# Two-block transformer kernel on one core: another order of the second block's projections and attention groups

## The chip, the cores and the metric

The kernel runs on one core of one Trainium2 chip. The metric is the device time of one execution in microseconds (us); lower is better. All weights come from HBM, every product runs on TensorE (PE), and VectorE (DVE), ScalarE (ACT), GpSimd (POOL) and the DMA queue of SyncE (SP) serve it.

## The reference

Two residual blocks on x of 512 tokens by 1024 features. The first block has a recurrent layer and a sliding-window attention layer; the change leaves its code as it is. The second block, cut to what matters:

```python
h = rms_norm(x, norm_mix) @ w_in                       # 1024 -> D_PROJ
# NSA, 4 heads: compressed, selected and window branch, gated sum
kv_c = gelu(windows(kv[0:2]) + pe, cmp_w1) @ cmp_w2    # 31 compressed keys and values
o = g0 * attn(q, kv_c) + g1 * attn(q, k_sel, v_sel) + g2 * attn(q, k_win, v_win)
# dilated, 2 heads: three groups of keys (every 1st, 4th, 16th), merged by denominators
# stick breaking, 6 heads, strictly causal:
z = q @ k.T * scale
after = reverse_cumsum(log_sigmoid(-z)) - log_sigmoid(-z)
a = exp(log_sigmoid(z) + after);  o = a @ v
x = x + concat(o_nsa, o_dil, o_stick) @ w_out
x = x + relu(rms_norm(x, norm_mlp) @ w_up) ** 2 @ w_down
```

## The kernel before, in words

**Units.** The weights are 173 units of 128 by 1024 floats, in the order in which PE uses them. SP loads unit u into slot u % 4 of a ring, from the first attention on POOL splits it into a high and a low part (`wh`, `wl`), and both wait until PE is done with unit u - 4. Every projection is a three-term product (high by high, high by low, low by high; lines L1017 to L1019). A feature-major tile (`F`, 128 features by 512 tokens) takes one unit and 24 matmuls; a token-major group (`G0` to `G4`, four token tiles) takes four units and 96 matmuls.

**Before the second attention.** PE goes through `G0` (NSA queries, keys, values), the sum of squares, `G1` (dilated queries and gates), the spread of the norm (L1076), `F0` (raw compressed keys), `G2` (dilated keys), `F1`, the hidden layer of the compression (`hid`, four units `U_W1` of short products), `F4`, the turn of the hidden layer (`hT`), six tiles of transposes of the NSA heads (`nT`), `G4` (stick values) and `kc`. Each result stands in one of 8 PSUM banks, and PE may write a bank once the tile before in it was read (`free`): by ACT, or, for `F` and `nT`, by DVE, whose low parts (L1998, L2001, L2020) come behind ACT's high parts (L1543, L1558). DVE normalises heads at L1980 (NSA, wanted by `nT`) and L1976 (dilated, `normalise`).

**The second attention** (`make_attention(2)`) runs over 68 groups of 128 queries: 24 stick groups, 4 compressed (`cmp`), 32 selected or window (`sel`, `win`), and last 8 dilated (`dil`). At step i each engine does a fixed list, in order. PE: `scores(i + 4)` (L666), `turn(i)` (transposes of the probabilities, L683), `values(i - 1)` (L705), a pair's turn (L715), and a piece of an item. ACT: `soft1(i + 3)`, `soft2(i + 2)`, its copies. DVE: `mask1(i + 3)` (L890, softmax kinds), `mask2(i + 2)` (L904, L905, L909, stick kinds), `copy_out(i)` (L822), `finish`, items. Scores have three banks in turn, transposes two, sums of values two. A softmax group needs one pass on DVE and one on ACT, a stick group three and four. `ITEMS2` lays pieces of other work between the steps: the tiles `F2`, `F5`, `F3`, `F6` (stick heads), `G3` (dilated values) and the six turns `dT` of dilated heads (L1298). All of them use bank 7, as the pairs' turns do.

The batches stand in the order stick pair 0, compressed, stick pair 1, NSA pair 0, stick pair 2, NSA pair 1, dilated; the output projection (`output_tile`) and the MLP follow.

Of the kernel before, what the change touches and what calls it, by code (L numbers as in the profile page):

```python
# [20 lines left out]
F32 = mybir.dt.float32  # L21
F32R = mybir.dt.float32r
ALU = mybir.AluOpType
# [3 lines left out]
P = 128  # L27
# [25 lines left out]
U_G1 = U_G0 + 4  # L53
U_F0 = U_G1 + 4
U_G2 = U_F0 + 1
U_F1 = U_G2 + 4
U_W1 = U_F1 + 1
U_F4 = U_W1 + 4
U_G4 = U_F4 + 1
U_FB = U_G4 + 4  # L60
U_FC = U_FB + 2
U_G3 = U_FC + 2
U_OUT2 = U_G3 + 4
# [18 lines left out]
def source_unit(u):  # L82
# [10 lines left out]
    if U_F1 <= u < U_F4:  # L93
        return u + 4 if u == U_F1 else u - 1
    if U_FC <= u < U_OUT2:
        return u + 4 if u < U_G3 else u - 2
# [15 lines left out]
for _name, _n in [("rg", NG * 3 * NRG), ("g_a", KD), ("g_kv", KD), ("g_b", KD), ("g_mix", KD), ("g_mlp", KD),  # L112
# [23 lines left out]
A_OT2, A_BIAS4, A_VC4, A_HIDT, A_BIASD = 12160, 13696, 14208, 14464, 14720  # L136
# [16 lines left out]
EVAC = {"gate": "D", "kcT": "A", "F": "D", "G3": "A", "dT": "A"}  # L153
# [6 lines left out]
MIX_TILE = {0: 10, 1: 2, 2: 6, 3: 0, 4: 9, 5: 11}  # L160
MIX_ORDER = (3, 4, 0, 5, 1, 2)
# [5 lines left out]
SLOT2 = (0, 1, 2, 1, 0, 2)  # L167


def plan():  # L170
# [8 lines left out]
    seg2 += [("G1", t, "A") for t in range(4)] + [("rstd", 2, "B"), ("F", 0, "D")]  # L179
    seg2 += [("G2", t, "A") for t in range(4)] + [("F", 1, "D"), ("hid", 0, "A"), ("hid", 1, "A"), ("F", 4, "D")]  # L180
    seg2 += [("hT", 0, "A")] + [("nT", j, "D") for j in range(6)] + [("G4", t, "A") for t in range(4)] + [("kc", 0, "A")]
    bank, free, before = {}, {}, {}
    count = {"A": 0, "D": 0}
    for seg, items in ((seg1, ITEMS1), (seg2, ITEMS2)):
        for i, (name, j, who) in enumerate(seg):
            key = (name, j)
            bank[key] = i % 8
# [7 lines left out]
            before[key] = free[seg[i - 8][:2]] if i >= 8 else None  # L195
# [5 lines left out]
    last = {i % 8: free[seg2[i][:2]] for i in range(len(seg2))}  # L201
# [3 lines left out]
def attention_one():  # L205

    batches = [dict(kind="swa", head=h, pair=h // 2, half=h % 2, last=h % 2 == 1,
                    turn=h // 2) for h in range(16)]
    groups = [dict(b=h, n=n, w=[128 if n == 0 else 256]) for h in range(16) for n in range(TB)]
    return batches, groups  # L210


def attention_two():
# [10 lines left out]
    batches = stick(0) + cmp_ + stick(1) + nsa(0) + stick(2) + nsa(1) + dil  # L224
    groups = []
    turn = 0
    for b, batch in enumerate(batches):
        batch["turn"] = turn
        turn += batch["last"]
        for n in range(batch["first"], batch["first"] + 2) if batch["kind"] == "cmp" else range(TB):  # L230
# [1950 lines left out]
```

## Time and profile before

| | us |
|---|---|
| median of 3 runs | 1229.95 (1229.75 to 1231.45) |
| profiled execution, own time | 1230.32 |
| its span | 1228.5 |
| PE busy | 1148.0 (93%) |
| DVE, POOL, ACT busy | 630.7, 490.8, 427.2 |

The span runs from the first to the last instruction; 1.8 us of the execution's time lie around it. Busy PE time counts an instruction's full duration, at whichever clock was granted, so a stretch at the lower clock looks busy and does half the work.

### The profile page before, as it was taken

The page shows a single profiled execution, that of the slowest core. Times are in us where ns is not written, and L with a number is a line of the kernel's source. Part 1 is how long each engine was busy: PE and PEld are TensorE (multiplying, and loading weights), DVE is VectorE, ACT ScalarE, POOL GpSimd, SP SyncE. Part 2 cuts the span into 40 slices and gives each one's busy share as a digit, 9 for nine tenths or more (in the row PEclk, how much of TensorE's full clock was granted, in tenths as well). Part 3 has the DMA queues.
Part 4 walks back from the last instruction along what each step waited for, and adds up shares of the span by engine and source line. Part 5 has one row for each costly group of instructions (what it writes and reads, how often), then busy time and mean ns, then how long its engine had stood idle before and what let it go on. Part 6 is the DMA issues. An engine that isn't in the chain of part 4 may idle for free. (4 is left out here: it accounts for less than half of the span.)

```text
span 1228.5 us, 16028 instructions
## 1 busy us (share of the span) xinstructions
PE 1148.0 (93%) x5777; PEld 972.7 (79%) x5777; DVE 630.7 (51%) x1121; ACT 427.2 (35%) x848; POOL 490.8 (40%) x489
## 2 busy tenths in 40 slices
PE   6999999999899989997888887999899999999998
PEld 5888888888788878895777876687688888888887
DVE  6869777585666727138377665334541231231221
ACT  5374586353365602122475554321220110110110
POOL 0000000001614329689521104005877777777772
PEclk9999999999999999998988988569899999999999
DMA  6323232323210103333210001001323323323221
GB/s 251 121 86 96 93 95 95 120 87 103 85 36 19 35 3 118 103 103 121 86 35 19 18 2 69 1 1 51 104 87 102 103 88 100 102 87 101 99 89 51
DMA packets 27277, 97.15 MB, mean 79 GB/s; under 512 B 3024, under 2 KB 3408, under 8 KB 27088
## 3 DMA queue, kind: packets, MB, share of 16 engines
q1 hardware_dynamic: 27216, 96.32, 23.7%
q8 instruction: 40, 0.66, 0.2%
q14 instruction: 21, 0.17, 0.0%
HBM read 94.21 MB, written 2.10 MB: 78 GB/s over the span
## 5 line engine op out<-in xcount | busy, mean ns | idle before, releaser
L476 POOL TENSOR_TENSOR hold<-hold 128x2 f32<-128x2 f32 x117 | 27.9, 238 | 662.9 <-PE bank L1019 662.9
L1017 PE MATMUL bank<-xh,wh 128*128 128x512 f32 x568 | 230.9, 406 | 20.5 <-DVE xl L1645 14.5
L1018 PE MATMUL bank<-xl,wh 128*128 128x512 f32 x568 | 224.6, 395 | 0.0
L1019 PE MATMUL bank<-xh,wl 128*128 128x512 f32 x568 | 224.4, 395 | 0.0
L1017 PE MATMUL bank<-yh,wh 128*128 128x512 f32 x520 | 205.2, 395 | 6.9 <-POOL wl L480 4.9
L1018 PE MATMUL bank<-yl,wh 128*128 128x512 f32 x520 | 204.2, 393 | 0.0
L1019 PE MATMUL bank<-yh,wl 128*128 128x512 f32 x520 | 204.2, 393 | 0.0
L480 POOL TENSOR_TENSOR wl<-raw,wh 128x512 fp32r<-128x512 f32 x117 | 175.3, 1499 | 0.0
L479 POOL TENSOR_TENSOR wl<-raw,wh 128x512 fp32r<-128x512 f32 x117 | 157.5, 1346 | 9.8
L1017 PEld LDWEIGHTS bank<-xh,wh 128*128 128x128 f32 x568 | 108.9, 192 | 45.3 <-issue 14.2
L1019 PEld LDWEIGHTS bank<-xh,wl 128*128 128x128 f32 x568 | 108.7, 191 | 23.4
L1018 PEld LDWEIGHTS bank<-xl,wh 128*128 128x128 f32 x568 | 109.1, 192 | 21.6 <-issue 0.7
L477 POOL TENSOR_SCALAR wh<-raw 128x1024 fp32r<-128x1024 f32 x117 | 125.0, 1068 | 0.0
L1017 PEld LDWEIGHTS bank<-yh,wh 128*128 128x128 f32 x520 | 98.7, 190 | 28.2 <-issue 7.8
L1018 PEld LDWEIGHTS bank<-yl,wh 128*128 128x128 f32 x520 | 98.9, 190 | 20.6
L1019 PEld LDWEIGHTS bank<-yh,wl 128*128 128x128 f32 x520 | 98.8, 190 | 20.8
L1609 ACT ACTIVATE arena<-arena 128x512 f32<-128x512 f32 x32 | 20.2, 633 | 247.3 <-DVE arena L2055 247.3
L1017 PE MATMUL bank<-wh,xh 128*128 128x512 f32 (+2 forms) x224 | 86.1, 385 | 15.6 <-DVE arena L1990 6.4
L705 PE MATMUL bank<-arena 128*128 128x64 f32 (+2 forms) x620 | 96.2, 290 | 3.5 <-ACT arena L796 2.0
L705 PEld LDWEIGHTS bank<-arena 128*128 128x128 f32 x620 | 91.9, 217 | 4.6 <-ACT arena L796 2.6
L2067 DVE TENSOR_TENSOR x<-bank,x 128x512 f32<-128x512 f32 x32 | 22.1, 692 | 142.0 <-PE bank L1019 142.0
L1676 DVE TENSOR_TENSOR wl<-raw,wh 128x1024 fp32r<-128x1024 f32 x56 | 68.0, 1222 | 40.0 <-ACT wh L1368 39.6
(235 smaller groups left out, 1803.8 us busy)
## 6 DMA issues: line engine op xcount, KB each, us to landing
raw<-weight_units SPq DMA_DIRECT2D x173, 512.0 KB, 3.4
x<-x_in SPq DMA_DIRECT2D x4, 512.0 KB, 7.8
out_fm<-x SPq DMA_DIRECT2D x8, 256.0 KB, 2.0
arena<-tables SPq DMA_DIRECT2D x1, 1024.0 KB, 11.4
par<-params SPq DMA_DIRECT2D x1, 166.0 KB, 2.4
arena<-swa_table SPq DMA_DIRECT2D x1, 128.0 KB, 12.0
ident<-identity SPq DMA_DIRECT2D x1, 64.0 KB, 9.2
```

The lines of the kernel that those rows point to most:

```text
L476: pool.tensor_tensor(hold[:], hold[:], hold[:], ALU.add).then_inc(held, 1)
L477: pool.tensor_scalar(wh[:, j, :], raw[:, j, :], 1.0, 1.0, ALU.mult, ALU.mult).then_inc(high_done, 1)
L479: pool.tensor_tensor(wl[:, j, 0:512], raw[:, j, 0:512], wh[:, j, 0:512], ALU.subtract)
L480: pool.tensor_tensor(wl[:, j, 512:1024], raw[:, j, 512:1024], wh[:, j, 512:1024], ALU.subtract)\
L705: mm = pe.matmul(out, pt[:, c % slots, j * P:(j + 1) * P], value_ap(g, s_, kb), start=first, stop=total == 0)
L1017: pe.matmul(out, lh, rh, start=start, stop=False)
L1018: pe.matmul(out, lh, rl, start=False, stop=False)
L1019: return pe.matmul(out, ll, rh, start=False, stop=stop)
L1609: act.activation(sq2[:, i % 2, :], up[:, i % 2, :], ACT.Square)
L1676: dve.tensor_tensor(wl[:, u % RING, :], raw[:, u % RING, :], wh[:, u % RING, :], ALU.subtract)\
L2067: dve.tensor_tensor(x[:, m, :], B[4 + m % 4][:], x[:, m, :], ALU.add).then_inc(down_read, 1)
```

## The change

It reorders the second block; no product is added or dropped.

- `F0` stands ahead of `G1`, and `F4` between the second and the third unit of the hidden layer. `hT` stands behind `nT`.
- `G3` takes the place of `G4` ahead of the attention, with `F2`, `F5`, `F3` behind it. `F6` and `G4` stand behind the scores of the first three groups (`behind_scores`). Only the turns `kcT` and `dT` are left in `ITEMS2`, `dT` at steps 22 to 32.
- DVE normalises the dilated heads (`r1`, `r2`) behind the low parts of `nT`, no longer between `F1` and `F4`.
- Six stick groups stand first; then stick and NSA groups take turns, two NSA or compressed groups for a stick group or one for one, and the dilated groups last. All stick batches sum in bank 5, the others in bank 6 (`bank_of`), with a count of finished batches for each bank.
- From step 1 on PE does `turn(i)` and `values(i - 1)` ahead of `scores(i + 4)`; DVE does `finish` ahead of `mask2`, ACT an item ahead of `soft2`.

```diff
-ITEMS2 = {-3: ("F", 2, 4), 1: ("kcT", 0, 1), 2: ("F", 5, 4), 14: ("F", 3, 4), 18: ("F", 6, 4),
-          27: ("G3", 0, 4), 33: ("G3", 1, 4), 41: ("G3", 2, 3), 44: ("G3", 3, 3),
-          49: ("dT", 0, 1), 50: ("dT", 1, 1), 51: ("dT", 2, 1), 52: ("dT", 3, 1), 53: ("dT", 4, 1), 54: ("dT", 5, 1)}
+ITEMS2 = {-1: ("kcT", 0, 1), 22: ("dT", 0, 1), 24: ("dT", 1, 1), 26: ("dT", 2, 1), 28: ("dT", 3, 1), 30: ("dT", 4, 1),
+          32: ("dT", 5, 1)}
...
-    seg2 += [("G1", t, "A") for t in range(4)] + [("rstd", 2, "B"), ("F", 0, "D")]
+    seg2 += [("F", 0, "D"), ("rstd", 2, "B")] + [("G1", t, "A") for t in range(4)]
     seg2 += [("G2", t, "A") for t in range(4)] + [("F", 1, "D"), ("hid", 0, "A"), ("hid", 1, "A"), ("F", 4, "D")]
-    seg2 += [("hT", 0, "A")] + [("nT", j, "D") for j in range(6)] + [("G4", t, "A") for t in range(4)] + [("kc", 0, "A")]
+    seg2 += [("nT", j, "D") for j in range(6)] + [("hT", 0, "A")] + [("G3", t, "A") for t in range(4)]
+    seg2 += [("F", 2, "D"), ("F", 5, "D"), ("F", 3, "D"), ("kc", 0, "A")]
+    seg2 += [("F", 6, "D")] + [("G4", t, "A") for t in range(4)]
...
-    batches = stick(0) + cmp_ + stick(1) + nsa(0) + stick(2) + nsa(1) + dil
+    batches = stick(0) + stick(1) + stick(2) + cmp_ + nsa(0) + nsa(1) + dil
...
+    groups, ahead = sticks[:6], 6
+    for k, group in enumerate(others):
+        groups.append(group)
+        while ahead < len(sticks) and (ahead - 6) * 33 < (k + 1) * 18 - 9:
+            groups.append(sticks[ahead])
+            ahead += 1
+    return batches, groups + dilated
...
                 for i in range(-LOOK - 1, ng + OUT_LAG):
-                    if 0 <= i + LOOK + 1 < ng:
+                    if (a == 1 or i < 1) and 0 <= i + LOOK + 1 < ng:
                         scores(i + LOOK + 1)
+                    if i == -2 and a == 2:
+                        behind_scores()
                     if 0 <= i < ng:
                         turn(i)
                     if 0 <= i - V_LAG < ng:
                         values(i - V_LAG)
+                    if a == 2 and i >= 1 and i + LOOK + 1 < ng:
+                        scores(i + LOOK + 1)
...
+            for q, u in enumerate(U_W1):
+                if q == 2:
+                    f_tile(4)
...
+            turn_hidden()
+            token_major(U_G3, 4, 384, "G3", xh, xl)
+            for j in (2, 5, 3):
+                f_tile(j)
...
+            def behind_scores():
+                f_tile(6)
+                token_major(U_G4, 4, 384, "G4", xh, xl)
```

On DVE, ahead of the attention, these rows stand in a row before; L1980 and L1976 normalise NSA and dilated heads, L1990 with L1998 or L2001 makes `F1` and then `F4`, L2020 are the low parts of `nT`:

```order
L1980 TENSOR_TENSOR arena<-arena,v 128x768 x4
L2005 TENSOR_REDUCE sides<-ident 128x2
L1990 SCALAR_TENSOR_TENSOR arena<-bank,rstd 128x512
L1998 TENSOR_TENSOR yl<-arena,yh 128x512
L1976 TENSOR_TENSOR arena<-arena,v 128x384 x8
L1990 SCALAR_TENSOR_TENSOR arena<-bank,rstd 128x512
L2011 CAST yh<-ident 128x128
L2012 CAST yh<-arena 128x128
L2001 SCALAR_TENSOR_TENSOR yl<-arena,sides,yh 128x512 x2
L2020 SCALAR_TENSOR_TENSOR yh<-bank,hsc,yh 64x512
```

The same place in the change, where the lines have the numbers L2063, L2073, L2081, L2084, L2099 and L2059 (dilated heads):

```order
L2063 TENSOR_TENSOR arena<-arena,v 128x768 x4
L2088 TENSOR_REDUCE sides<-ident 128x2
L2073 SCALAR_TENSOR_TENSOR arena<-bank,rstd 128x512
L2081 TENSOR_TENSOR yl<-arena,yh 128x512
L2073 SCALAR_TENSOR_TENSOR arena<-bank,rstd 128x512
L2084 SCALAR_TENSOR_TENSOR yl<-arena,sides,yh 128x512 x2
L2099 SCALAR_TENSOR_TENSOR yh<-bank,hsc,yh 64x512
L2099 SCALAR_TENSOR_TENSOR yl<-bank,hsc,yl 64x512
L2099 SCALAR_TENSOR_TENSOR yl<-bank,par,yh 128x512 x2
L2101 CAST yh<-ident 128x128
L2102 CAST yh<-arena 128x128
L2059 TENSOR_TENSOR arena<-arena,v 128x384 x8
```

The eight operations on dilated heads moved behind everything that `F4` and `nT` wait for.

On PE, two steps of the attention before, in NSA groups with a piece of `F` between them (L666 scores, L683 transposes, L705 values, L1017 to L1019 the piece in bank 7):

```order
L666 MATMUL bank1<-yh 128x256
L666 MATMUL bank1<-yl,yh 128x256
L683 MATMUL bank4<-ident,arena 128x128 x2
L705 MATMUL bank5<-arena 128x64
L1017 MATMUL bank7<-xh,wh 128x512
L1018 MATMUL bank7<-xl,wh 128x512
L1019 MATMUL bank7<-xh,wl 128x512
...
L666 MATMUL bank2<-yh 128x384
L666 MATMUL bank2<-yl,yh 128x384
L683 MATMUL bank3<-ident,arena 128x128 x3
L705 MATMUL bank5<-arena 128x64 x2
```

Two steps of the change (L762 transposes, L782 values, L745 and L748 scores):

```order
L762 MATMUL bank3<-ident,arena 128x128 x2
L782 MATMUL bank5<-arena 128x64
L745 MATMUL bank0<-yh 128x384
L745 MATMUL bank0<-yl,yh 128x384
L745 MATMUL bank0<-yh,yl 128x384
L748 MATMUL bank0<-yh 128x128
L762 MATMUL bank4<-ident,arena 128x128 x3
L782 MATMUL bank6<-arena 128x64 x2
L745 MATMUL bank1<-yh 128x128
L745 MATMUL bank1<-yl,yh 128x128
```

The scores moved behind the transposes and values of their step, stick and NSA steps take turns, and nothing stands between the steps.

## Rows read from the trace of the kernel before

**Rows 1.** The page: span, busiest engines, granted clock in 40 slices.

```profile
span 1228.5 us, 16028 instructions
...
PE 1148.0 (93%) x5777; PEld 972.7 (79%) x5777; DVE 630.7 (51%) x1121; ACT 427.2 (35%) x848; POOL 490.8 (40%) x489
...
PEclk9999999999999999998988988569899999999999
```

**Rows 2.** Busy time by stretch; columns as the first line names them.

```profile
core 0: us, PE busy (x) PEld busy (x) DVE busy (x) ACT busy (x) POOL busy (x), PEclk, DMA share, GB/s
504.00:528.00 24.00, 21.03 (x110) 20.34 (x108) 5.62 (x11) 4.66 (x14) 15.23 (x18) 0.93 0.27 88
...
556.00:604.00 48.00, 36.97 (x344) 33.47 (x343) 31.47 (x34) 9.32 (x17) 39.59 (x38) 0.86 0.32 100
604.00:763.40 159.40, 130.76 (x822) 119.90 (x821) 102.64 (x279) 92.34 (x250) 34.09 (x35) 0.90 0.10 34
699.00:718.00 19.00, 17.51 (x131) 16.74 (x131) 16.04 (x37) 15.64 (x38) 0.00 (x0) 1.00 0.01 1
763.40:826.00 62.60, 59.01 (x229) 45.69 (x230) 24.13 (x81) 18.76 (x59) 0.00 (x0) 0.56 0.00 1
```

**Rows 3.** Waits of PE from 500 to 764 us: total, times, longest.

```profile
PE bank L666 <- DVE arena L909: 8.4, 5, 3.1
PE bank L1017 <- DVE arena L1990: 7.3, 2, 6.4
PE bank L1298 <- DVE yl L986: 4.6, 1, 4.6
PE bank L1017 <- DVE yl L986: 4.2, 1, 4.2
PE bank L1017 <- ACT arena L1496: 3.0, 1, 3.0
...
PE bank L1017 <- POOL wl L480: 2.5, 1, 2.5
```

**Rows 4.** Timeline of PE: end of `G4`, and a piece of `F2`.

```profile
603.06 0.33 PE L1018 MATMUL bank<-wl,xh 128*128 128x384 f32 x1
603.23 0.34 PE L1019 MATMUL bank<-wh,xl 128*128 128x384 f32 x1
...
605.20 0.40 PE L1018 MATMUL bank<-xl,wh 128*128 128x512 f32 x1
605.43 0.39 PE L1019 MATMUL bank<-xh,wl 128*128 128x512 f32 x1
```

**Rows 5.** Timeline of DVE ahead of `nT` and `G4`: start, duration.

```profile
561.45 6.58 DVE L1980 TENSOR_TENSOR arena<-arena,v 128x768 f32<-128x768 f32 x4
...
568.26 0.69 DVE L1990 SCALAR_TENSOR_TENSOR arena<-bank,rstd 128x512 f32<-128x512 f32 x1
...
570.90 9.80 DVE L1976 TENSOR_TENSOR arena<-arena,v 128x384 f32<-128x384 f32 x8
580.62 0.68 DVE L1990 SCALAR_TENSOR_TENSOR arena<-bank,rstd 128x512 f32<-128x512 f32 x1
...
582.70 2.63 DVE L2001 SCALAR_TENSOR_TENSOR yl<-arena,sides,yh 128x512 fp32r<-128x512 f32 x2 [0.74 <-ACT yh L1543]
585.37 0.76 DVE L2020 SCALAR_TENSOR_TENSOR yh<-bank,hsc,yh 64x512 fp32r<-64x512 f32 x1
```

**Rows 6.** Groups of DVE from 604 to 763.4 us: busy, mean ns.

```profile
L2001 DVE SCALAR_TENSOR_TENSOR yl<-arena,sides,yh 128x512 fp32r<-128x512 f32 x4 | 3.1, 816 | 2.1 <-ACT yh L1543 2.1
...
L1990 DVE SCALAR_TENSOR_TENSOR arena<-bank,rstd 128x512 f32<-128x512 f32 x4 | 2.7, 681 | 0.0
...
L1998 DVE TENSOR_TENSOR yl<-arena,yh 128x512 fp32r<-128x512 f32 x2 | 2.5, 1252 | 0.3 <-ACT yh L1543 0.3
```

**Rows 7.** Busy time in two stretches at the lower clock (columns of rows 2).

```profile
746.50:753.30 6.80, 4.40 (x19) 4.21 (x20) 3.64 (x8) 2.00 (x5) 4.45 (x5) 0.50 0.38 114
766.90:821.50 54.60, 52.07 (x176) 39.34 (x175) 19.88 (x69) 17.05 (x56) 0.00 (x0) 0.50 0.00 0
```

**Rows 8.** Timeline of PE, the wait ahead of a fall of the clock.

```profile
688.19 1.34 PE L705 MATMUL bank<-arena 128*128 128x64 f32 x6 [1.52 <-DVE arena L822]
```

More of the change, by code:

```diff
@@ L194, in plan @@
                 free[key] = (who, j + 1)
-            before[key] = free[seg[i - 8][:2]] if i >= 8 else None
+            earlier = [k for k in (item[:2] for item in seg[:i]) if bank[k] == bank[key]]
+            before[key] = free[earlier[-1]] if earlier else None
         for key in (item[:2] for item in items.values()):
@@ L199, in plan @@
             free[key] = (EVAC[key[0]], count[EVAC[key[0]]])
-    last = {i % 8: free[seg2[i][:2]] for i in range(len(seg2))}
+    last = {bank[item[:2]]: free[item[:2]] for item in seg2}
     return bank, free, before, last
 def attention_one():
-    batches = [dict(kind="swa", head=h, pair=h // 2, half=h % 2, last=h % 2 == 1,
-                    turn=h // 2) for h in range(16)]
+    batches = [dict(kind="swa", head=h, pair=h // 2, half=h % 2, last=h % 2 == 1) for h in range(16)]
     groups = [dict(b=h, n=n, w=[128 if n == 0 else 256]) for h in range(16) for n in range(TB)]
@@ L710, in pair_turn @@
                 def pair_turn(p):
-                    pe.wait_ge(s["fin"], groups[pairs[p]]["b"] + 1)
+                    for b, batch in enumerate(batches):
+                        if batch["pair"] == pair_of[p] and (batch["last"] or batch["kind"] == "dil"):
+                            pe.wait_ge(*fin_of(b))
                     if before7[("pair", p)]:
@@ L822, in pt_copy @@
                 copy(pt[:, c % slots, 0:n], B[3 + c % 2][:, 0:n]).then_inc(s[("pt_even", "pt_odd")[c % 2]], 1)
-            def stick_count(i):
-                return sum(1 for g in groups[:i] if batches[g["b"]]["kind"] == "stick")
             def dve_part(dve, link, item):
                 def bias_part(at, w):
-                    return ar({256: A_BIASD, 768: A_BIAS4}[at], w) if at >= 256 else bias[:, at:at + w]
+                    return ar({256: A_BIASD, 768: A_ST}[at], w) if at >= 256 else bias[:, at:at + w]
                 def make_bias(b):
@@ L917, in finish @@
                     b = batches[bi]
-                    kind, p = b["kind"], b["turn"]
+                    kind, p = b["kind"], turn_of[bi]
                     ended = end_of[bi] + 1
@@ L926, in finish @@
                         dve.wait_ge(s["o_done"], ended)
-                        nsa_turns = [batches[groups[i]["b"]]["turn"] for i in pairs if batches[groups[i]["b"]]["kind"] == "win"]
+                        nsa_turns = [pair_of.index(j) for j in range(2)]
                         for j, turn in enumerate(nsa_turns):
@@ L990, in dve_part @@
                         mask1(i + LOOK)
+                    if a == 2 and 0 <= i - FIN_LAG < ng and i - FIN_LAG == end_of[groups[i - FIN_LAG]["b"]]:
+                        finish(groups[i - FIN_LAG]["b"])
+                    if a == 2 and i in (0, 2):
+                        item(("F", ("scale", "low")[i // 2]))
                     if 0 <= i + LOOK - 1 < ng:
@@ L1551, in _ @@
             stick_high(4)
+            for j in range(6):
+                wait_done(act, ("nT", j))
+                act.activation(q_stack(j) if j < 4 else side((KS_TILE, KW_TILE)[j - 4], 0), B[BANK[("nT", j)]][:], ACT.Copy,
+                               scale=hsc[:, 1:2] if j < 4 else gain("nsa", j - 2)).then_inc(turned_high, 1)
             wait_done(act, ("hT", 0))
```

322 lines of the change are left out of this document (176 added, 146 removed).

## The prediction, made before the run

> **What bounds the kernel now.** I read the page first. PE is busy 93% of the span, and the row of its clock is full but for a dip in slices 18 to 27, about 560 to 830 us [rows 1]. So almost everywhere only less PE work would help, and this change takes none away; it can gain only inside the dip. The busy times by stretch come next [rows 2]. Before 763.4 us, the second attention has PE busy for 130.8 of 159.4 us at a mean clock of 0.90, DVE for 102.6, ACT for 92.3. The 48 us ahead of it have PE busy for 37.0 at 0.86. The dilated groups that follow keep PE busy for 59.0 of 62.6 us, but at 0.56. The waits say who is late [rows 3]: mostly DVE, with 8.4 us for stick groups (L909), 6.4 us for the bank that `F4` holds (L1990), and 4.6 and 4.2 us for bank 7 (L986), where a turn or a piece of `G3` stands in PE's queue with ready work behind it.
>
> Two costs follow: PE's idle time, and the half clock after it. The last wait of [rows 8], 1.52 us, is followed by such a stretch. No engine is saturated in the attention before: PE's work at full clock is 130.8 x 0.90 = 118 us of 159.4, and DVE stands at 64%.
>
> **The change part by part.** All times below are on the profiled execution's axis.
>
> *F0 ahead of G1.* Before, `G1` waits 3.0 us for a bank of `G0` that ACT empties (L1496) [rows 3], and the stretch from 504 to 528 us runs at a clock of 0.93, so 24 x 0.07 = 1.7 us more are lost [rows 2]. `F0` is 24 matmuls at 0.23 us (the step between two starts in [rows 4]), 5.5 us, which lie over the 3.0. `F0` needs nothing from ACT. I take 4.5 us; bounds 3.0 and 4.7.
>
> *F4 inside the hidden layer.* The 2.5 us wait for POOL's split [rows 3] goes: `F4` gives POOL 5.5 us in the middle of four units that PE uses up fast. But PE then meets `nT` sooner, which waits for L1980. That ended at 568.0 [rows 5], so at 563.5 now. The 2.5 are therefore no gain of their own; what counts is DVE's chain.
>
> *Normalising of the dilated heads moved.* Before, its 9.8 us (L1976) stood between the F1 and the F4 work, and `G4` waited for F4's bank [rows 5]. It now runs under `G3`, 16.6 us of PE (96 matmuls at the 0.17 us step of [rows 4]), with the wide `F` tiles behind it. What is late next: `G3`'s second tile needs the bank of the first `nT` tile, whose low part is queued on DVE behind F1 and F4. From 563.5 that queue is: F1's part 2.6 us (568.26 to 570.90), F4's 4.7 (580.62 to 585.33), one low part 0.8, and 0.3 for L2005: 571.9 [rows 5]. `G3` ends at 571.9 + 16.6 = 588.5, and I add 2.4 for the half clock after a wait of some 5 us: 590.9. `G4`, which stood there before, ended at 603.5 [rows 4]. Gain so far 12.6 us, the 4.5 included. Bounds: without the clock's loss 15; with the whole 48 x 0.14 = 6.7 us of it as before [rows 2], 8.
>
> *The pieces moved out of the loop.* Before, four `F` tiles (22 us) and `G3` (16.6) lay between steps, 38.6 us. Now `F2`, `F5`, `F3`, then `F6` and `G4` are one block: 16.5 + 5.5 + 16.6, with about 2 us for `kc` and the first three groups' scores, 40.6 us. The first turn is at 590.9 + 40.6 = 631.5. POOL's splitting keeps up, as it has over 5 us for an `F` unit.
>
> *The loop.* From there 56 steps lead to the first dilated scores, which stood at 763.4. PE's work for all 60 groups is 118 - 39 = 79 us at full clock, 74 for these steps, 1.3 us a step. DVE's is 102.6, less 8.3 for the `F` tiles [rows 6], plus 2.3 for `F6` (one of four L1990, half of L2001), less about 4.5 for three narrow stick groups done under the block (eight stick groups keep DVE busy 16.0 us from 699 to 718 [rows 2]), plus 1.5 for finishing work that comes earlier: 93.6 us. So DVE, not PE, is the bound, and the pieces that covered DVE's lateness are gone: they no longer hide anything but were 38.6 us of PE's path. How well can DVE be used? Lower end: as now, 64%, which makes 146 us. The stretch from 699 to 718, eight stick groups in a row, has 16.04 of 19 us, 84% [rows 2]. Upper end 95%, 98 us. In the new order the three passes of a stick group lie beside softmax groups, whose passes need no ACT between them; and PE's transposes, for which DVE's copies wait, no longer stand behind scores that wait for a bank. I take 86%, just above the stick stretch: 109 us.
>
> The start costs extra. ACT empties `G4`'s four banks and makes F6's high parts before it can touch group 3, and groups 3 to 5 are stick groups in a row. I estimate 4 us (0 to 8). And PE at 1.3 us of work in a step of 1.95 is 68% busy; some of the time the clock will be at half. In such a stretch PE needs 2.6 us a step, 0.65 over DVE's. If a quarter of the steps are so, 14 x 0.65 = 9, of which DVE's own waits absorb part: I take 5 (0 to 18). First dilated scores at 631.5 + 4 + 109 + 5 = 749.5, against 763.4: 13.9 us gained, where 12.6 had been gained ahead of the block.
>
> *Dilated groups and after.* The same work, at the same clock of 0.50 [rows 7]. PE idles 62.6 - 59.0 = 3.6 us there; with turns and values ahead of the scores some is covered: 1.5. The output projection is unchanged.
>
> *New waits.* All NSA batches sum in bank 6, so a batch's first values wait for the `finish` of the batch before, behind which the next scores are queued; before, batches alternated over two banks. There are nine such places. The nearest row is PE's 1.52 us wait for a DVE copy [rows 8]: between 0 and 14 us. PE has slack of 0.65 us a step and DVE is working during those waits, so I count it inside the 86%.
>
> Sum: 13.9 + 1.5 = 15.4 us off 1230.3, 1214.9; the median of the runs shown is 0.4 below the profiled one, so 1214.5, and I say **1214**.
>
> **The rule that speaks against it.** In the dilated stretch PE is busy for 52.1 of 54.6 us and stays at 0.50, so the level of 1.2 GHz, all the way [rows 7]. Its work is fp32 scores, transposes and fp32 values. The loop loses its dense projection pieces and becomes mostly transposes and values as well. The Trainium skill, "TensorE: Matmul & The Clock Gate", Part 4, says that a transpose does not count as PE-busy in the same way for the clock. By that rule the whole loop could sit at 1.2 GHz, 148 us; by my reading of the rows it does not, 109 + 5. Against the rule: from 746.5 to 753.3 PE had only turns, scores, transposes and values, was idle for 2.4 us of it, and the clock came back to full behind it [rows 7].
>
> **Rivals.**
> 1. *The loop turns slow (slower than before).* PE's 74 us at a mean clock c take 74 / c. From 635.5 to 764.9 there are 129 us, so the change loses as soon as c falls under 0.57. At 0.50: 635.5 + 148 = 783.5, 20 us late, less 1.5: 1248. The same comes about if DVE stays at 64%: 635.5 + 146. For it: the dilated stretch, and 68% busy. Against it: the mean of 0.90 now with 18% idle, and a PE at half clock is fully busy again. Chance 0.16.
> 2. *The waits for `finish` are all paid.* Nine times 1.5 us on the path: 14 of the 15 us are gone, 1228. For it: one bank for each kind. Chance 0.05.
> 3. *DVE nearly saturated and the clock holds.* 631.5 + 2 + 98 = 731.5, 32 us earlier, 1196; if the dilated groups also stayed at full clock, up to 20 us below that, but nothing in the rows points to it. Chance 0.18.
> 4. *My forecast*, 1206 to 1226: chance 0.61.
>
> **How the numbers follow.** A measurement of this kernel tells about 0.2%, 2.5 us, from no change: 1227.5 to 1232.4. Faster by more: 0.61 + 0.18 = 0.79. Same: 0.05. Slower: 0.16. The range is 1199 to 1234: it holds the forecast, the nearer part of rival 3, rival 2 and the mildest slow cases. The forecast's own range is 1206 to 1226.
>
> **What would show it.** In the profile after: no wait of 3.0 us for L1496; the wait ahead of the second group after `nT` shorter than 6.4 us and put down to a low part of `nT`; the first transposes of probabilities at about 631; no projection matmul until the dilated groups; the first 64-row scores at about 750; DVE at 80 to 90% in between, and the clock above 0.8. A mean clock below 0.6 or DVE below 70% would make me wrong towards slower; a first 64-row score before 740 towards faster.

## The result, and the profile after

| | before | after |
|---|---|---|
| median, same chip | 1230.70 (1229.75 to 1233.00, 4 runs) | 1244.66 (1243.99 to 1247.33, 4 runs) |
| ratio | | 1.0118, 95% interval 1.0075 to 1.0160 |
| profiled span | 1228.5 | 1245.5 |

The change makes the kernel 1.2% slower, some 14 us; 1214 had been predicted. The page of the kernel after (compare [rows 1]; the dip of its clock is deeper, not wider):

```profile
span 1245.5 us, 16005 instructions
PE 1166.5 (94%) x5777; PEld 988.1 (79%) x5777; DVE 631.4 (51%) x1121; ACT 424.4 (34%) x847; POOL 492.6 (40%) x489
PEclk9999999999999999999977786559899999999999
```

The work is the same, yet PE is 18.5 us busier: its matmuls lasted longer. Busy time by stretch says where (columns of [rows 2]; the fourth row is the loop, from the first transposes of probabilities to the first 64-row scores):

```profile
504.00:528.00 24.00, 24.00 (x127) 22.49 (x126) 12.28 (x19) 4.88 (x14) 19.10 (x19) 1.00 0.28 92
571.70:605.90 34.20, 34.16 (x166) 31.04 (x167) 19.18 (x20) 4.40 (x10) 31.76 (x31) 0.95 0.37 123
605.90:632.10 26.20, 25.92 (x145) 24.40 (x146) 8.70 (x19) 9.81 (x25) 21.19 (x22) 1.00 0.32 102
632.10:783.40 151.30, 113.66 (x613) 102.78 (x612) 89.36 (x256) 78.53 (x220) 2.50 (x2) 0.74 0.02 7
783.40:844.10 60.70, 59.12 (x229) 45.88 (x228) 25.31 (x81) 17.81 (x58) 0.00 (x0) 0.55 0.00 1
```

Everything ahead of the loop went as planned: PE has no gap from 504 to 528 us and 0.3 us of gaps from 571.7 to 632.1. The timeline of PE shows the one long new wait of the front, the first `F2` matmul, the first transposes of probabilities and the first 64-row scores:

```profile
571.74 0.69 PE L1102 MATMUL bank<-wh,xh 128*128 128x384 f32 x1 [3.57 <-DVE yh L2099]
...
589.38 0.39 PE L1102 MATMUL bank<-xh,wh 128*128 128x512 f32 x1
...
632.10 0.51 PE L762 MATMUL bank<-ident,arena 128*128 128x128 f32 x3
...
783.43 1.43 PE L745 MATMUL bank<-arena 64*128 64x128 f32 x5
```

`G3` ends at 589.4 (590.9 forecast), the loop begins at 632.1 (631.5 forecast). Then 151.3 us pass where 118 had been forecast; before, the first 64-row scores stood at 763.4 [rows 2], now at 783.4. In the loop PE idles for 151.3 - 113.7 = 37.6 us, at a mean clock of 0.74, and DVE is busy for 59% of it. Its longest waits, all engines (total, times, longest):

```profile
DVE arena L973 <- PE bank L745: 33.0, 20, 3.8
ACT arena L875 <- DVE arena L992: 29.0, 20, 3.5
ACT arena L857 <- DVE negm L973: 27.0, 27, 2.5
PE bank L782 <- ACT arena L880: 18.8, 10, 4.5
DVE arena L908 <- PE bank L762: 18.1, 4, 14.1
...
PE bank L782 <- DVE arena L908: 10.1, 7, 2.0
```

DVE's `mask1` (L973) waits for scores (L745), ACT's `soft2` (L875) for DVE's `mask2` (L992), PE's value products (L782) for the copy of ACT (L880) or of DVE (L908): a ring, in which everybody waits. (Of the 18.1 us of L908 for L762, 14.1 are one wait.) One turn of the ring, in the timelines of PE, ACT and DVE:

```profile
684.04 0.38 PE L762 MATMUL bank<-ident,arena 128*128 128x128 f32 x2
688.88 0.66 PE L782 MATMUL bank<-arena 128*128 128x64 f32 x2 [4.46 <-ACT arena L880]
689.30 0.45 PE L745 MATMUL bank<-yh 128*128 128x128 f32 x1
```

```profile
684.22 0.19 ACT L857 ACTIVATION_READ_ACCUMULATOR arena<-arena,negm 128x1 f32 x1
687.94 0.63 ACT L875 ACTIVATE arena<-arena 128x512 f32<-128x512 f32 x1 [3.53 <-DVE arena L992]
688.47 0.26 ACT L880 ACTIVATE arena<-bank 128x128 f32<-128x128 f32 x1
```

```profile
684.77 0.42 DVE L1048 TENSOR_TENSOR arena<-arena 128x256 f32<-128x256 f32 x1
685.23 0.69 DVE L987 SCALAR_TENSOR_TENSOR arena<-bank,arena 128x512 f32<-128x512 f32 x1
685.95 1.22 DVE L988 TENSOR_TENSOR_SCAN arena<-ones,arena 128x512 f32<-128x512 f32 x1
687.21 0.69 DVE L992 TENSOR_TENSOR arena<-bank,arena 128x512 f32<-128x512 f32 x1
...
692.61 0.29 DVE L973 CUSTOM_DVE_ANT_0 arena<-bank,arena 128x128 f32<-128x128 f32 x1 [3.31 <-PE bank L745]
```

PE's transposes are done at 684.4. Their copy by ACT (L880) is ready to run then, but it is queued behind `soft2` (L875) of a stick group two ahead, which waits for DVE's three passes (L987 to L992). So the value products start at 688.9, and the scores behind them, which need none of this, are 4.5 us late too, and with them those of the next step, a softmax group. For these DVE then waits 3.3 us, until 692.6.

### The profile page after: what moved, and what is told of

It reads as the page before. It is cut to its first block and busy times, and to the rows that moved or that the text cites. A ratio compares the mean times of both kernels' runs of the same rounds, so it can differ in the third digit from the quotient of the medians.

```text
span 1245.5 us, 16005 instructions
## 1 busy us (share of the span) xinstructions
PE 1166.5 (94%) x5777; PEld 988.1 (79%) x5777; DVE 631.4 (51%) x1121; ACT 424.4 (34%) x847; POOL 492.6 (40%) x489
## 5 line engine op out<-in xcount | busy, mean ns | idle before, releaser
L1102 PE MATMUL bank<-xh,wh 128*128 128x512 f32 x568 | 227.6, 401 | 16.9 <-DVE xl L1728 15.0
L782 PE MATMUL bank<-arena 128*128 128x64 f32 (+2 forms) x620 | 108.9, 316 | 35.0 <-ACT arena L880 18.8
L782 PEld LDWEIGHTS bank<-arena 128*128 128x128 f32 x620 | 102.1, 238 | 42.4 <-issue 12.9
L857 ACT ACTIVATE arena<-arena,negm 128x128 f32<-128x128 f32 (+3 forms) x120 | 61.2, 510 | 82.0 <-DVE negm L973 81.4
```

Source lines behind the costliest of these rows:

```text
L782: mm = pe.matmul(out, pt[:, c % slots, j * P:(j + 1) * P], value_ap(g, s_, kb), start=first, stop=total == 0)
L857: e = act.activation(pr[:, col:col + w], pr[:, col:col + w], ACT.Exp, scale=-1.0, bias=negm[:, ring_of[g["b"]], n:n + 1], accum_out=to_sum)
L1102: pe.matmul(out, lh, rh, start=start, stop=False)
```

## The experiments

The changed kernel differs from the one before in four main things: the front, the pieces (in the loop or ahead of it), the order of the groups, and the order of a step. With them go a bank for each kind of group and the place of `finish` and of an ACT item. **The theory (A)**: scores behind value products close the ring above. **Rivals**: (B) PE's clock is low without dense pieces, whatever the order; (C) the mixed order of the groups is to blame; later (D), the step order harms only where mixed groups meet a loop without pieces.

"Loop" runs from the first transposes or values to the first 64-row scores, "dilated" from there to the output projection, both in the profiled execution; "idle" is the loop less PE's busy time in it. Ratios are against the kernel before on the same chip. Kernels marked "in" keep `F2`, `F5`, `F3`, `F6`, `G3` and `dT` as pieces, "out" have them as the change has. "Batch, out" keeps one bank for all stick batches and one for the others; "batch, in" has the two banks in turn, as before.

| kernel | groups, pieces, scores | median us | ratio (95%) | loop, PE busy, idle, clock | dilated |
|---|---|---|---|---|---|
| before | batch, in, first | 1230 to 1234 | 1 | 146.9, 121.3, 25.6, 0.90 | 63.0 |
| after | mixed, out, last | 1244.7 | 1.0118 (1.0075 to 1.0160) | 151.3, 113.7, 37.6, 0.74 | 60.7 |
| e1 | mixed, out, first | 1225.0 | 0.9941 (0.9918 to 0.9965) | 126.4, 99.7, 26.7, 0.80 | 62.9 |
| e2 | mixed, out, middle | 1220.7 | 0.9867 (0.9786 to 0.9948) | 125.2, 101.7, 23.5, 0.79 | 61.7 |
| e3 | batch, out, last | 1229.1 | 0.9985 (0.9969 to 1.0000) | 131.8, 100.0, 31.8, 0.83 | 61.5 |
| e4 | after + dense products | 1253.5 | 1.0190 (1.0158 to 1.0223) | 154.6, 122.7, 31.9, 0.85 | 61.4 |
| e5 | after, copies first | 1238.9 | 1.0068 (1.0035 to 1.0101) | 146.4, 112.7, 33.7, 0.73 | 54.1 |
| e6 | batch, in, first, new front | 1209.4 | 0.9856 (0.9792 to 0.9921) | 143.6, 119.3, 24.3, 0.92 | 56.7 |
| e7 | before with scores last | 1213.6 | 0.9864 (0.9813 to 0.9915) | 148.0, 126.4, 21.6, 0.88 | 45.4 |
| e8 | mixed, in, first | 1206.0 | 0.9813 (0.9756 to 0.9869) | 145.5, 118.1, 27.4, 0.93 | 56.6 |
| e9 | mixed, in, last | 1223.5 | 0.9927 (0.9899 to 0.9954) | 159.5, 132.1, 27.4, 0.85 | 61.3 |
| e10 | batch, in, last, new front | 1198.3 | 0.9718 (0.9689 to 0.9746) | 147.9, 122.8, 25.1, 0.91 | 45.3 |
| e11 | batch, out, first | 1215.8 | 0.9853 (0.9806 to 0.9900) | 126.7, 101.6, 25.1, 0.78 | 55.7 |
| e12 | before, last in dilated only | 1215.1 | 0.9849 (0.9807 to 0.9891) | 150.6, 126.8, 23.8, 0.86 | 45.4 |
| e13 | e6, last in dilated only | 1197.1 | 0.9747 (0.9684 to 0.9811) | 144.1, 120.3, 23.8, 0.92 | 43.7 |
| e14 | e1, last in dilated only | 1226.9 | 0.9946 (0.9903 to 0.9988) | 136.4, 110.6, 25.8, 0.71 | 55.9 |
| e15 | e8, last in dilated only | 1211.6 | 0.9836 (0.9767 to 0.9905) | 143.9, 120.2, 23.7, 0.93 | 60.9 |
| e16 | e13, middle in the loop | 1195.3 | 0.9722 (0.9661 to 0.9784) | 142.9, 120.6, 22.3, 0.92 | 45.1 |
| e17 | after, finish behind | 1257.3 | 1.0242 (1.0136 to 1.0347) | 159.4, 120.6, 38.8, 0.67 | 61.1 |
| e18 | e15, finish behind | 1221.1 | 0.9936 (0.9895 to 0.9977) | 158.2, 129.9, 28.3, 0.86 | 54.4 |

The kernels were timed in five lots: e1, e3, e4, e6; e2, e5, e7, e8; e9 to e12; e13 to e16; e17 and e18. The kernel before had medians from 1230.1 to 1234.3 in them, so a difference of medians from two lots is open by some 4 us; that holds for most of the small ones below. How much one trace's loop may vary is seen in four pairs that have the same loop program: before and e12 (146.9, 150.6), e6 and e13 (143.6, 144.1), e8 and e15 (145.5, 143.9), e1 and e14 (126.4, 136.4). Only the last is far apart, and its idle time agrees (26.7, 25.8): the 10 us are matmuls that took longer, at a mean clock of 0.71 in place of 0.80. The verdicts below go by medians; the loops say where the time lies.

**e1_scores_first**: the changed kernel with the old step order.

```diff
-                    if (a == 1 or i < 1) and 0 <= i + LOOK + 1 < ng:
+                    if 0 <= i + LOOK + 1 < ng:
                         scores(i + LOOK + 1)
...
-                    if a == 2 and i >= 1 and i + LOOK + 1 < ng:
-                        scores(i + LOOK + 1)
```

> The changed kernel, but PE does scores(i + 4) ahead of turn(i) and values(i - 1) in every step, as the kernel before did. Theory A (the new order of a step couples the engines: values(i - 1) wait for a copy queued behind soft2 or mask2, and the scores that DVE needs next stand behind them): the 33 us that DVE waits for scores shrink below 10, the first 64-row scores come 15 to 30 us earlier than 783, the time falls from 1245 to 1215 to 1230. Theory B (the lost clock: without dense projection pieces PE works at 1.2 GHz in much of the loop): the loop stays within 5 us of now, mean clock still about 0.75, 1240 to 1248. Theory C (the mixed order of the groups does not suit the queues): no change either, 1240 to 1248.

1225.0 us, 20 less than the changed kernel. Its loop by stretch, and its waits:

```profile
631.80:758.20 126.40, 99.66 (x598) 91.59 (x596) 88.11 (x254) 76.34 (x218) 1.72 (x2) 0.80 0.02 7
```

```profile
ACT arena L873 <- DVE arena L990: 28.1, 20, 3.1
PE bank L745 <- DVE arena L990: 17.4, 14, 3.0
```

Against the loop of after, 24.9 us are gone: 10.9 of idle time, 14.0 of busy time, which are the same matmuls at a higher clock. DVE's `mask1` no longer waits for scores at all; ACT's for `mask2` has not changed. PE does wait again for a score bank, the wait that the new step order was to remove, but it costs less.

**e3_batch_order**: the changed kernel, step order kept, groups in the old order of batches.

```diff
-    groups, ahead = sticks[:6], 6
-    for k, group in enumerate(others):
...
+    per = [groups_of(b) for b in range(16)]
+    groups = [g for b in (0, 1, 6, 7, 2, 3, 8, 9, 10, 11, 4, 5, 12, 13, 14, 15) for g in per[b]]
```

> The changed kernel with the groups in the order of the kernel before (stick pair 0, compressed, stick pair 1, NSA pair 0, stick pair 2, NSA pair 1, dilated), all else as changed. Theory C: 1215 to 1232, the loop from 632 to the first 64-row scores falls from 151 to below 135 us. Theories A and B: the stick batches in a row make DVE's chain longer, 1245 to 1260.

1229.1 us, 15.6 less. So with the scores last the mixed order costs nearly as much as the step order does, and the two are not separate terms: that called for the other combinations.

**e4_dense**: the changed kernel with two more products of 512 columns ahead of the scores of groups 4 to 59, without the four compressed ones. What they write is overwritten.

```diff
+                        if a == 2 and kind != "dil" and i > 3:
+                            for _ in range(2):
+                                pe.matmul(score_bank(st)[:], idm[:, 0, :], yh[:, 2, :], start=True, stop=True)
```

> The changed kernel with two extra products of 128x512 (fp32r, about 0.43 us at full clock) into the score bank ahead of each group's scores from group 4 to the last NSA group; their result is overwritten, so the output is that of the changed kernel. It adds 56 x 0.43 = 24 us of PE work at full clock. Theory B: the clock in the loop rises from 0.75 to above 0.9 and the time stays or falls, 1232 to 1247. Theory A: the waits stay and the added work stands in front of the scores, 1250 to 1270, with the clock higher all the same.

104 products at the 0.23 us step of [rows 4] are 23.9 us of work, for 8.9 us of time:

```profile
630.80:785.40 154.60, 122.69 (x710) 108.36 (x710) 88.47 (x251) 76.63 (x216) 1.30 (x2) 0.85 0.01 5
```

The clock rose from 0.74 to 0.85, PE's busy time by only 9 us, its idle time fell by 5.7. Over 60% of the added work paid for itself. The run does not say that the clock is harmless, it says that the ring stays when the clock rises.

**e6_front_alone**: the kernel before with the new front, that is `F0` ahead of `G1`, `F4` inside the hidden layer, `nT` ahead of `hT`, the dilated heads normalised behind.

```diff
-    seg2 += [("G1", t, "A") for t in range(4)] + [("rstd", 2, "B"), ("F", 0, "D")]
+    seg2 += [("F", 0, "D"), ("rstd", 2, "B")] + [("G1", t, "A") for t in range(4)]
...
-            normalise(r1, 6)
-            normalise(r2, 12).then_inc(heads_normed, 1)
...
+            normalise(r1, 6)
+            normalise(r2, 12).then_inc(heads_normed, 1)
```

> The kernel before with only the part ahead of the attention changed: F0 ahead of G1, F4 inside the hidden layer, hT behind nT, the dilated heads normalised behind the low parts of nT; G4 stays there, the loop is that of before with all its pieces. By my sum the part ahead gains 12.6 us (the changed kernel's trace agrees: its first turn is at 632.1 where I had 631.5), so 1215 to 1221. If the loop's start then waits for the normalising instead (9.8 us of DVE now behind nT), half of it comes back: 1221 to 1226.

1209.4 us: the front was worth more than forecast. `kc` ends at 588.1 where it ended at 604.2, 16 us earlier; the rest lies mostly in the dilated section (56.7 after 63.0). Its four runs lie between 1204.4 and 1219.7, so the size is loose.

**e2_scores_mid**: the changed kernel, step order turn(i), scores(i + 4), values(i - 1).

```diff
-                    if 0 <= i - V_LAG < ng:
-                        values(i - V_LAG)
                     if a == 2 and i >= 1 and i + LOOK + 1 < ng:
                         scores(i + LOOK + 1)
+                    if 0 <= i - V_LAG < ng:
+                        values(i - V_LAG)
```

> The changed kernel with a step's order on TensorE turn(i), scores(i + 4), values(i - 1): the scores stand behind the transposes but ahead of the value products. Theory A (the new step order couples the engines: the scores of the group four ahead stand behind value products that wait for ScalarE's or VectorE's copy of the turned probabilities, and both of these engines then wait for those scores): the wait of the values for the copies no longer holds the scores, so most of the 20 us between the changed kernel and the one with its scores first come back, 1225 to 1232 us. Theory B (the loop is long because TensorE's clock is low when transposes and values stand together): the transposes are apart from the values again, loop clock near 0.80 as with the scores first, time 1225 too; it differs from A only if the clock and the time part ways. Theory A2 (it is the transposes ahead of the scores that do the harm, not the values): about 1240 us, little won.

1220.7 us, 24 less than the changed kernel and no more than with the scores first. Its four runs lie between 1204.0 and 1223.6, and its profile is of the slowest; all are at least 20 us under the changed kernel. DVE's wait for scores is 9.0 us here, after 33.0. Transposes ahead of the scores do no harm: it is the value products, which wait for the copies, that must not stand ahead of them.

**e5_copies_first**: in the changed kernel, ACT and DVE copy the turned probabilities ahead of `soft2`, `finish` and `mask2`.

```diff
+                    if a == 2 and 4 <= i < 56:
+                        copy_out(i)
                     if 0 <= i + LOOK - 1 < ng:
                         soft2(i + LOOK - 1)
```

> The changed kernel, TensorE's order as it is, but in steps 4 to 55 ScalarE and VectorE copy the turned probabilities of group i before their soft2, finish and mask2 of other groups. Theory A (the values wait because those copies are queued behind soft2 and mask2, which wait for each other): the waits of L782 for the copies (18.8 + 10.1 us in the loop of the changed kernel) fall under 12 us together, and 8 to 15 us of the time come back, 1230 to 1237 us. Theory B (clock): no product is changed, so the clock is not either, and the time stays within 3 us of 1244.7. Theory C (the copies wait for the transposes now, so what was queued behind them is late instead): 1240 to 1250 us, with a wait of ScalarE's and VectorE's copies for L762 in place of L782's wait.

1238.9, 6 us of the 20. The ring is loosened at another place; PE's idle time falls by 3.9, and `mask1` waits for scores still for 26.4 us.

**e7_before_scores_last**: the kernel before with the new step order alone.

```diff
-                    if 0 <= i + LOOK + 1 < ng:
+                    if (a == 1 or i < 1) and 0 <= i + LOOK + 1 < ng:
                         scores(i + LOOK + 1)
...
+                    if a == 2 and i >= 1 and i + LOOK + 1 < ng:
+                        scores(i + LOOK + 1)
```

> The kernel before, with only the step order on TensorE changed from step 1 on: turn(i), values(i - 1), then scores(i + 4). Units, pieces and the order of the batches stay. Theory A (step order alone couples the engines): slower by 10 to 25 us, 1241 to 1256, with long waits of the value products for copies and of VectorE and ScalarE for score banks. Theory C (the step order only hurts together with the mixed order of the groups; in batch order it cost little in the changed kernel): within 5 us of 1231. Theory B (clock): slower only by as much as the loop's mean granted clock falls from before's.

1213.6, 1.4% faster, which none of the three had. The loop is as long as it was (148.0 after 146.9), as theory C had it; what changed is the dilated section, 45.4 after 63.0.

**e8_all** and **e9_mixed_pieces_last**: e6 with the mixed groups, their banks and `finish` ahead of `mask2`, the pieces kept in the loop (some at other steps); scores first in e8, last in e9.

> The kernel before with the new front (F0 ahead of G1, W1 and F4 interleaved, turns of the NSA heads ahead of the hidden layer's) and the mixed order of stick and sparse groups with its banks, but with the scores first in each step as before and with F2, F5, F3, F6, G3 and the dilated turns kept as pieces in the loop. The front alone gave 1209.4 us. If mixing the groups evens out VectorE's and ScalarE's load (as the prediction had it), it gives 3 to 15 us more: 1194 to 1206. If the mixed order gives nothing because the pieces already filled the waits: 1207 to 1212. If it harms (waits for score banks of mask2 at every other step): 1213 to 1225.

> The kernel with the new front, mixed groups and the pieces kept in the loop (1206.0 us with its scores first, first 64-row scores at 747.0), and now the new step order: scores(i + 4) behind turn(i) and values(i - 1), in front of the piece. Theory A (the new step order harms wherever groups are mixed): first 64-row scores 15 to 25 us later, 762 to 772. Theory D (it harms only where mixed groups meet a loop without pieces, since a piece gives the copies their time before the next values): first 64-row scores within 4 us of 747. The time itself also hangs on how long the dilated section's half clock lasts.

1206.0 and 1223.5: mixing the groups won 3 us over e6, which these intervals do not tell from nothing. The step order on top cost 17.5 by the medians, which are from two lots, and 14 by the ratios and by the loops:

```profile
601.50:747.00 145.50, 118.12 (x766) 107.29 (x764) 98.15 (x260) 77.85 (x220) 32.04 (x31) 0.93 0.09 30
```

```profile
601.00:760.50 159.50, 132.10 (x780) 119.02 (x778) 98.61 (x259) 79.80 (x221) 31.84 (x32) 0.85 0.08 27
```

Here the idle time is 27.4 in both, and the whole 14 us are busy time, the same matmuls at a lower mean clock. The pieces do not save the mixed loop, so theory D falls. The waits of e9 show the ring again; in e8 `mask1` never waits for scores:

```profile
ACT arena L859 <- DVE arena L974: 32.5, 20, 3.6
DVE arena L955 <- PE bank L731: 24.8, 18, 3.2
```

**e10_front_scores_last**: e6 with the new step order, the same edit as in e7.

> The kernel before with the new front alone (1209.4 us with its scores first, first 64-row scores at 745.7, 56.7 us from there to the output projection), and now the new step order. In the kernel before the new step order alone left the loop as long as it was (616.5 to 764.6) and shortened the dilated section from 63.0 to 45.3 us. If both parts add: first 64-row scores at 747, output projection 45 to 57 us later, 1194 to 1207 us. If the gain in the dilated section was chance: 1207 to 1212.

1198.3, 11 us under e6, in the dilated section. In this loop, in batch order, `soft2` waits for `mask2` half as often as in e9:

```profile
ACT arena L779 <- DVE negm L896: 37.1, 28, 4.4
DVE arena L896 <- PE bank L670: 17.1, 17, 3.2
ACT arena L797 <- DVE arena L915: 15.1, 10, 2.5
```

**e11_batch_scores_first**: e3 with the scores first.

> The changed kernel with the groups in the batch order of before and its scores first in each step: of the change only the front, with the pieces out of the loop, is left. With the new step order this order of groups had its first 64-row scores at 762.9 (131.8 us of loop), and with scores first the mixed order had them at 758.2 (126.4). Theory D (step order harms only mixed groups without pieces): within 4 us of 762.9, so mixing alone gives 4 to 5 us where scores stand first. Theory A (step order harms in any order): 750 to 758.

1215.8, 13 us under e3: 5.1 in the loop, all of it idle time and more, 5.8 in the dilated section. The loop's end (760.7) is where theory D had it, and yet the step order cost something here too: batch order without pieces is not safe from it.

**e12_last_in_dilated**, **e13_front_last_in_dilated**, **e14_e1_last_in_dilated**, **e15_all_last_in_dilated**: before, e6, e1 and e8, each with scores last from step 55 on only.

```diff
-                    if 0 <= i + LOOK + 1 < ng:
+                    if (a == 1 or i < 55) and 0 <= i + LOOK + 1 < ng:
...
+                    if a == 2 and i >= 55 and i + LOOK + 1 < ng:
+                        scores(i + LOOK + 1)
```

> The kernel before, with the new step order only for the scores of the eight dilated groups (steps 55 on). Putting every group's scores last gave 1213.6, all of it between the first 64-row scores and the output projection (63.0 to 45.3 us). If that gain comes of the step order in the dilated section itself: 1211 to 1218 us, that stretch under 52 us. If it comes of the clock that the loop ahead leaves, or of chance: 1225 to 1235 us, that stretch 60 to 64 us.

> The kernel before with the new front (1209.4 us; loop 143.7 us with scores first, 147.9 with scores last; dilated section 56.7 and 45.3 us) and the new step order only for the scores of the eight dilated groups. If loop and dilated section are separate terms: first 64-row scores at 745.7, output projection 45 us later, 1192 to 1197 us, the best so far. If the dilated section is short only behind a loop that has scores last too: 1205 to 1212.

> The changed kernel with its scores first (1225.0 us, 62.9 us from the first 64-row scores to the output projection), and the new step order only for the dilated groups. If the step order in the dilated section is what keeps the clock up there: that stretch 45 to 50 us and 1208 to 1213 us. If the clock at entry decides (mixed loop without pieces, TensorE short of work ahead of it, as in the changed kernel's 60.6 us with the same order): 60 to 63 us, 1222 to 1227 us.

> New front, mixed groups, pieces in the loop, scores first (1206.0 us, dilated section 56.6 us), with the new step order only for the dilated groups. With scores last throughout that stretch was 61.3 us. If the step order in the dilated section decides: 45 to 50 us, 1194 to 1200. If the clock at entry decides, and this loop leaves it as the one with scores last did: 57 to 62 us, 1206 to 1212.

1215.1, 1197.1, 1226.9 and 1211.6. Behind the batch loops the dilated section shrinks to 45.4 and 43.7 us; behind the mixed ones the same step order leaves it at 55.9 and 60.9. The dilated stretch of e13 and of e15:

```profile
747.50:791.20 43.70, 40.43 (x225) 32.17 (x224) 24.06 (x81) 18.35 (x59) 0.00 (x0) 0.84 0.00 1
```

```profile
746.80:807.70 60.90, 57.92 (x228) 44.71 (x227) 26.01 (x84) 18.60 (x59) 0.00 (x0) 0.58 0.00 1
```

The same work, 17.5 us of busy time apart. At the start of the stretch, PE's waits in e13 and in e15, whose clock fell at 751.2 and stayed at 0.50 for 51.2 us:

```profile
751.35 0.66 PE L709 MATMUL bank<-arena 128*128 128x64 f32 x4 [0.40 <-ACT arena L802]
```

```profile
748.76 0.41 PE L768 MATMUL bank<-arena 128*128 128x64 f32 x2 [0.70 <-DVE arena L890]
749.87 1.67 PE L731 MATMUL bank<-arena 64*128 64x256 f32 x6 [0.71 <-DVE mtmp L955]
```

**e16_front_mid_then_last**: e13 with the step order of e2 in the loop.

> New front, batch order, pieces in the loop; the loop's steps are turn(i), scores(i + 4), values(i - 1), those of the dilated groups have scores last. Scores last throughout gave a loop of 147.9 us and 1198.3; scores first a loop of 143.7. If only scores behind values cost something, and transposes ahead of scores help: loop 138 to 144 us, 1186 to 1196. If transposes ahead of scores cost as much: loop 147 to 149, 1196 to 1200.

1195.3, the lowest median of all, but with e13 (1197.1) and e10 (1198.3) inside what these runs can tell. All three beat both kernels, by 2.5 to 2.8% of before.

**e17_finish_behind** and **e18_e15_finish_behind**: after and e15 with `finish` back behind the copies on DVE.

```diff
-                    if a == 2 and 0 <= i - FIN_LAG < ng and i - FIN_LAG == end_of[groups[i - FIN_LAG]["b"]]:
-                        finish(groups[i - FIN_LAG]["b"])
...
-                    if a == 1 and 0 <= i - FIN_LAG < ng and i - FIN_LAG == end_of[groups[i - FIN_LAG]["b"]]:
+                    if 0 <= i - FIN_LAG < ng and i - FIN_LAG == end_of[groups[i - FIN_LAG]["b"]]:
                         finish(groups[i - FIN_LAG]["b"])
```

> The changed kernel (1244.7 us), with finish on VectorE back behind copy_out, as before. If finish ahead of mask2 is what makes soft2 and the copies behind it late (1.5 us of five operations at 683.7 to 685.2, ahead of mask2's 2.7 us), the loop gets 5 to 15 us shorter: 1230 to 1240. If the mixed order and the scores behind the values do it, finish is only moved in a row that is late anyway: within 4 us of 1244.7; slower if the values of the next batch then wait longer for fin.

> New front, mixed groups, pieces in the loop, scores first but last in the dilated section (1211.6 us, 61.0 us from the first 64-row scores to the output projection), with finish behind the copies. If finish's place makes the dilated section slow: 44 to 50 us there and 1195 to 1200 us. If the clock that the mixed loop leaves at its end does: 57 to 62 us there, 1206 to 1214 us.

Both got slower, by 12.6 and 9.6 us. `finish` ahead of `mask2` is a gain in the mixed order, where a batch's first values wait for the bank of the batch before. With it behind, this wait of e17 grows from 3.4 us in the changed kernel:

```profile
PE bank L782 <- DVE arena L1048: 17.6, 6, 4.5
```

So the new place of `finish` does not explain the cost of the mixed order or of the step order.

## Why the prediction was wrong

**Ahead of the loop it was right.** The wait for L1496 is gone and the stretch from 504 to 528 runs at full clock; the new wait stood where it was named, 3.57 us on a low part of `nT`; `G3` ended 1.5 us sooner than forecast, the loop began 0.6 us later. The front's gain had been put at 12.6 us (bounds 8 to 15). By the end of `G3` it is 14.1 (603.5 to 589.4), inside them. In e6, with `G4` in that place, it is 16.1 (604.2 to 588.1 at the end of `kc`), a little more.

**The step that failed is the loop**, "86% ... 109 us", and in it the sentence that "PE's transposes ... no longer stand behind scores that wait for a bank". That was counted as a gain, and what the move queued behind the value products was not costed. Value products wait for copies, copies for `soft2`, `soft2` for `mask2`; with the scores behind them `mask1` waits as well. In the changed kernel this is worth 20 us (e1), with pieces in the loop 14 to 17.5 (e9 against e8). Its place is shown by e2, in the mixed order without pieces: the scores may stand behind the transposes, not behind the values. DVE was at 59%, not 86%, and below 70% was the prediction's own sign of being wrong towards slower. With the scores first it is 88.1 of 126.4 us, 70%, so 86% was too high even then.

**The mixed order was counted as a help, and with it the step order costs most.** In batch order with the pieces in, the step order in the loop costs 1.2 us by medians and 3.8 by the loops (e10 against e13); in mixed order 11.9 and 15.6 (e9 against e15). Batch order is not free of it where the pieces are out: there the step order, in the loop and the dilated section together, costs 13 us, of which 5.1 in the loop (e3 against e11). The rows fit: `soft2` waits for `mask2` 20 times in after, e1, e8 and e9, and 9 to 13 times in the batch orders. That more such waits are the cause was argued from them, not tried by itself. Scores first, mixing gains nothing that can be measured with the pieces in (e8 against e6), and loses 9 us with the pieces out (e1 against e11), most of it behind the loop.

**The pieces were not "38.6 us of PE's path".** Taken out of the mixed loop they shorten it by 19.1 us only (145.5 to 126.4), and of the 23.9 us of e4's products 8.9 were paid. In the loop such work fills waits and keeps the clock up (0.93 against 0.80). Ahead of the loop it costs its full time: e1 is 19 us slower than e8, both with scores first.

**The clock term** was 5 us, 0 to 18. Between the loops of after and e1 14.0 of 24.9 us are slower matmuls, between e9 and e8 all 14. So much of what the step order costs is paid through the clock. That rival B alone, a low clock without dense pieces, is not the cause is shown by e1 and e2: they have no pieces either, and are 20 and 24 us faster than the changed kernel. How the same idle time comes with a lower clock in e9 than in e8 stays open. Rival 1 is what came about in time and nearly in its second form, "if DVE stays at 64%": it gave 783.5 or 781.5 for the first 64-row scores and 1248, and 783.4 and 1244.7 were measured. Its first form, a mean clock under 0.57, did not happen (0.74). The waits for `finish` of rival 2 came to 5.5 us of the 14 (3.4, 1.4 and 0.7). The rule weighed there (the Trainium skill, "TensorE: Matmul & The Clock Gate", Part 4: a transpose does not count as busy time in the same way), read as strictly as the prediction read it, would have put the whole loop at 1.2 GHz; the trace shows a mix of both levels in every loop without pieces, with means of 0.67 to 0.85. e4 leaves the rule possible as a part of the cause: dense products raised the clock, but they also filled idle time, so it doesn't tell one from the other.

**The sum** of the steps from before to after, by the first 64-row scores of the profiled executions: front -17.7 (e6), mixed groups +1.4 (e8), pieces out +11.2 (e1), step order +25.3 (after), in all +20.0; by medians 1231, 1209.4, 1206.0, 1225.0, 1244.7. The step order had been forecast as a gain and the moved pieces as nearly neutral, and what the front gave hid half of the loss. The dilated stretch, where 1.5 us were forecast as gained, took 60.7 us after 63.0.

**What stays open** is the clock of the dilated section. With its own scores last it kept the full clock for 22 to 25 us behind the batch loops with pieces (e7, e10, e12, e13, e16); in every other kernel the clock had fallen by some 5 us after the first 64-row scores. All this is one profiled execution of each kernel; the single runs of e6 (1204.4 to 1219.7) and e2 leave room for either course in the same program. Short waits at its start, 0.70 and 0.71 us against 0.40, stand ahead of the fall in e15; no run changed them alone. e18, at 54.4 us, lies between. The bank for each kind and the place of the ACT item were tried only together with other parts of the change, so their shares of the steps above are not known.

## What to carry to other kernels

A move that takes one wait away must be costed by what then stands behind the next one. Where engines wait for each other in a ring, do not put what the others wait for (here the scores) behind something that itself waits (here the value products). This is no rule for every loop: in batch order with pieces the scores last cost next to nothing in the loop and came with a much shorter dilated section. Dense independent work between the steps of a loop that waits cost a good third to a half of its time here, and all of it ahead of the loop, so take it out only if the waits are gone. When several changes meet in one queue, measure the combinations: the step order was worth -17 us (e7) to +20 us (after against e1), depending on the order of the groups and the place of the pieces.

## What the runs showed of the hardware

- The same 225 to 230 PE instructions of the dilated section took 43.7 us at a mean clock of 0.84 and 60.9 at 0.58. Once the clock had fallen near its start it stayed at half for 41 to 61 us, PE busy for 95% of that in the kernel before [rows 7]; only in e5 and e18 did it come back after 20.5 us. Where it had not fallen, the same stream held it for 22 to 25 us.
- The same loop program ran 126.4 and 136.4 us in two kernels (e1, e14) with nearly the same idle time (26.7, 25.8) and mean clocks of 0.80 and 0.71. Ten runs of e1 spread from 1219.0 to 1227.5 us, with mean clocks of the whole run between 0.941 and 0.954.
- 23.9 us of added dense products in a loop that waits lengthened the kernel by 8.9 us; the loop's mean clock rose from 0.74 to 0.85 (e4).
